# Sums of squares ahead of the input projections moved from GpSimd to TensorE, and all residual additions to VectorE

## The reference

```python
def rmsnorm(x, g):
    xf = x.astype(jnp.float32)
    y = xf * lax.rsqrt(jnp.mean(xf * xf, axis=-1, keepdims=True) + RMS_EPS)
    return (y * g.astype(jnp.float32)).astype(x.dtype)
...
    for i in range(DEPTH):
        hn = rmsnorm(x, norm_mix_pre[i])
...
        x = x + rmsnorm(m, norm_mix_post[i])
        hn = rmsnorm(x, norm_ffn_pre[i])
        f = conv_ffn(hn, ffn_w_up[i], ffn_conv_w[i], ffn_conv_b[i], ffn_w_down[i])
        x = x + rmsnorm(f, norm_ffn_post[i])
```

## Time and profile before

| | us |
|---|---|
| median of 3 runs | 1633.6 (1633.12 to 1633.71) |
| the profiled execution | 1633.11 |
| its span, first to last instruction | 1631.3 |
| mean granted TensorE clock | 0.958 of 2.4 GHz |
| boundary 0: first product to the norm's broadcast | 10.65 to 26.16 |
| boundary 1: first product to the norm's broadcast | 552.74 to 572.80 |
| boundary 2: first product | 945.51 |
| boundary 3: first product to the norm's broadcast | 1233.30 to 1253.34 |

### The profile page before, as it was taken

The page is one execution under the profiler, slowest core; times in us unless marked ns, Lnnn a source line. Parts: engine busy times, 40 slices in busy tenths (PEclk is TensorE's granted clock), DMA queues, the critical chain, the costliest instruction groups (busy, mean ns, idle before and its releaser), DMA issues.

```text
span 1631.3 us, 20778 instructions
## 1 busy us (share of the span) xinstructions
PE 1495.3 (92%) x6774; PEld 1183.5 (73%) x6774; DVE 1020.8 (63%) x1443; ACT 585.4 (36%) x832; POOL 460.9 (28%) x236
## 2 busy tenths in 40 slices
PE   6799888988699799999999979999796999999996
PEld 5577676776588578888888757777574888888885
DVE  6888888889830587777800067777608877875002
ACT  5433344333432332232222235556434223223221
POOL 4333334334345500000044552322064000000453
PEclk9899999999899899999999989999898999999998
DMA  4333231332112122322322212211021232223221
GB/s 140 120 107 113 103 128 52 116 116 103 65 65 95 47 91 90 103 90 90 107 94 98 74 39 78 65 64 64 13 90 39 91 101 91 90 95 109 89 92 66
DMA packets 36271, 142.02 MB, mean 87 GB/s; under 512 B 4048, under 2 KB 4176, under 8 KB 34192
## 3 DMA queue, kind: packets, MB, share of 16 engines
q1 hardware_dynamic: 36240, 141.62, 25.1%
HBM read 139.38 MB, written 2.23 MB: 87 GB/s over the span
## 4 chain that ended last, share of the span: by engine, by line
PE 65%; DVE 17%; issue 12%; POOL 3%; ACT 2%; DVEq 1%; DMA 0%; SPq 0%; POOLq 0%; ACTq 0%
PE bank L353 20%; PE bank L354 20%; PE bank L355 20%; DVE cv_s L650 4%; POOL w_lo L322 3%; DVE cv_s L644 2%; DVE m_t L942 2%; DVE hn_lo L531 2%; DVE mbuf L539 1%; DVE x L555 1%; PE b_x L741 1%; PE b_y L666 1%; DVE ug_s L641 1%; PE b_y L669 1%; ACT w_hi L316 1%
## 5 line engine op out<-in xcount | busy, mean ns | idle before, releaser
L322 POOL TENSOR_TENSOR w_lo<-raw,w_hi 128x1024 fp32r<-128x1024 f32 (+1 forms) x125 | 325.3, 2602 | 1055.2 <-ACT w_hi L316 1055.2
L353 PE MATMUL bank<-hn_hi,w_hi 128*128 128x512 f32 x1288 | 526.5, 409 | 41.5 <-DVE hn_lo L531 32.9
L354 PE MATMUL bank<-hn_lo,w_hi 128*128 128x512 f32 x1288 | 516.0, 401 | 0.0
L355 PE MATMUL bank<-hn_hi,w_lo 128*128 128x512 f32 x1288 | 515.5, 400 | 0.0
L316 ACT ACTIVATE w_hi<-raw 128x1024 fp32r<-128x1024 f32 (+1 forms) x217 | 239.9, 1106 | 540.8 <-PE bank L355 534.8
L353 PEld LDWEIGHTS bank<-hn_hi,w_hi 128*128 128x128 f32 x1288 | 247.3, 192 | 116.6 <-issue 30.5
L355 PEld LDWEIGHTS bank<-hn_hi,w_lo 128*128 128x128 f32 x1288 | 246.2, 191 | 59.9
L354 PEld LDWEIGHTS bank<-hn_lo,w_hi 128*128 128x128 f32 x1288 | 247.2, 192 | 56.2
L387 DVE RECIPROCAL rcol<-root 128x4 f32<-128x4 f32 x24 | 4.1, 173 | 378.5 <-ACT root L375 368.6
L355 PE MATMUL bank<-h_hi,w_lo 128*128 128x512 f32 x352 | 139.2, 396 | 0.0
L353 PE MATMUL bank<-h_hi,w_hi 128*128 128x512 f32 x352 | 139.2, 396 | 0.0
(11 more groups left out here) (185 smaller groups left out, 1796.5 us busy)
## 6 DMA issues: line engine op xcount, KB each, us to landing
raw<-w_up SPq DMA_DIRECT2D x88, 512.0 KB, 3.2
raw<-w_mix SPq DMA_DIRECT2D x49, 512.0 KB, 3.2
raw<-w_dn SPq DMA_DIRECT2D x32, 704.0 KB, 4.0
raw<-w_qkv SPq DMA_DIRECT2D x24, 512.0 KB, 3.3
acs_bc<-scratch SPq DMA_DIRECT2D x8, 1024.0 KB, 4.7
ecs_bc<-scratch SPq DMA_DIRECT2D x8, 1024.0 KB, 6.7
raw<-w_sout SPq DMA_DIRECT2D x16, 512.0 KB, 3.2
raw<-w_aout SPq DMA_DIRECT2D x8, 512.0 KB, 3.3
```

Of the source, the lines that this page charges most:

```text
L322: nc.gpsimd.tensor_tensor(w_lo[:, slot, 0:ph.width], raw[:, slot, 0:ph.width], w_hi[:, slot, 0:ph.width].bitcast(F32), ALU.subtract).then_ ...
L353: nc.tensor.matmul(acc[:], wh, hi, start=first, stop=False)
L354: nc.tensor.matmul(acc[:], wh, lo, start=False, stop=False)
L355: return nc.tensor.matmul(acc[:], wl, hi, start=False, stop=last)
```

## The change

In boundaries 0 to 3 the squares of the pre norm are no longer added up by GpSimd. Each chunk's squares go straight to TensorE: `chunk_stat` makes four matmuls of one column with `sq` as weights and adds their results up in the bank `b_cb`. It stands behind the six products of its chunk, except for chunk 7, where it stands ahead of them. `sq_added`, for which ScalarE's squares wait, now rises there, on TensorE. The root reads `b_cb`. `POOL_ADDS` is empty for boundaries 1 to 3, so VectorE makes all eight additions to x; in boundary 4 it stays as it was. TensorE's wait for the last chunk of x moves from ahead of the sum to just ahead of the broadcast. The sums of the post norms stay.

```diff
-        def norm_root(act, n):
+        def norm_root(act, n, stat=b_norm):
             act.wait_ge(stat_ready, n + 1)
-            nc.scalar.activation(root[:], b_norm[:, 0:NB], ACT.Sqrt, bias=eps[:]).then_inc(root_ready, 1)
+            nc.scalar.activation(root[:], stat[:, 0:NB], ACT.Sqrt, bias=eps[:]).then_inc(root_ready, 1)
...
+        def chunk_stat(pe, name, m):
+
+            pe.wait_ge(sq_ready, KC * sum_no[name] + m + 1)
+            for b in range(NB):
+                last = nc.tensor.matmul(b_cb[:, b:b + 1], sq[:, m % 2, b * P:(b + 1) * P], mean_col[:, 0:1],
+                                        start=m == 0 and b == 0, stop=m == KC - 1 and b == NB - 1)
+            last.then_inc(sq_added if m < KC - 1 else stat_ready, 1)
...
-        POOL_ADDS = {b: (1, 3, 5) for b in range(1, 4)}
+        POOL_ADDS = {b: () for b in range(1, 4)}
         POOL_ADDS[4] = (1, 3, 5, 6)
...
             for c in range(KC):
                 if c == KC - 1:
-                    if b:
-                        wait_x_scaled(pe, b)
-                    sum_stat(pe, f"pre{b}")
+                    chunk_stat(pe, f"pre{b}", c)
                 pe.wait_ge(hnlo_ready, KC * b + c + 1)
                 for j in range(2):
                     last = product(acc_of(nxt, j), slot_of(nxt, j), c, hn_hi[:, c, :], hn_lo[:, c, :],
                                    c == 0, c == KC - 1)
                     if c == KC - 1:
                         last.then_inc(unit_done, 1)
+                if c < KC - 1:
+                    chunk_stat(pe, f"pre{b}", c)
+            if b:
+                wait_x_scaled(pe, b)
             norm_bcast(pe, norm_no[f"pre{b}"])
...
-            norm_root(act, norm_no[f"pre{b}"])
+            norm_root(act, norm_no[f"pre{b}"], b_cb)
...
             for m in range(KC):
                 if b and m in POOL_ADDS[b]:
                     add(m)
-                if nxt is not None and m:
-                    add_square(pool, f"pre{b}", m - 1, m - 1)
```

## The result

The median of the changed kernel is 1645.0 us (6 runs, 1641.0 to 1646.4), that of the kernel before 1633.9 us in the same comparison: a ratio of 1.0061, interval 1.0047 to 1.0075. The profiled execution took 1644.46 us, 11.4 us more than that of before (1633.11), and its spans differ by as much. It is slower, but by a sixth of the 68.8 us that were forecast.

A forecast was written before the change was run, and what follows sets the result against it. TensorE bounds boundary 0; VectorE, slowed by GpSimd, is last in the others at the fast clock. Slow-clock terms 17.8 + 3 x 13.2 + 4 x 2.1 + 3 x 1.0 = 68.8 us more gave 1702.4 us, range 1641 to 1712.

The forecast's parts named there:

- the case given 0.62: Boundaries 0 to 3: the clock, slow at each start, stays slow until the last chunk; 1702.4 us, own range 1677 to 1710.
- rival 1: Boundaries 0 to 3: clock rises as before; boundary 0 +5.3 us, the others 1.5 each, 1643.4 us in total; chance 0.16.
- the 3.85 us of the sum: Boundaries 1 to 3: TensorE's waits at the fast clock, which the added blocks would fill, 3.85 us in each.
- the term of 3.0 for the slow clock: Boundary 1 before the change: what the first 6.0 us at the slow clock cost, taken as 3.0 us.
- The price of a block: Four one-column matmuls between products on TensorE: 0.89 us at the fast clock, up to 1.7 at the slow one.
- Six products alone did not raise it: Ahead of the last attention products: clock 0.50 throughout 9.2 us, with six slow products, a wait and a longer run.
- The other reading, of the one-column matmuls at boundary 4: Boundary 4: after 1.9 us of them and 1.29 us idle the next matmul is slow, so they seem to weigh little or nothing.
- the terms of 17.8 and 3 x 13.2 us: Added loop time at the slow clock: 17.8 us in boundary 0 and 13.2 us in each of boundaries 1 to 3.
- the slow chunk 7, the slow broadcasts (1.10 us) and the slow units behind them: Slow clock at loop ends: chunk 7 1.1 us more, broadcast 1.0, each boundary; next unit 1.0 behind boundaries 1 to 3.
- 31.8 us: Each changed loop, first product to the one behind the last sum: slow products and start 18.1, blocks 10.2, pair 3.5.
- rival 2: Clock rises midway in some of the four boundaries and then stays up: 1643 to 1702 us, middle 1673; chance 0.13.
- Rival 4: Blocks nearly free at 0.1 us each, TensorE's waits in boundaries 1 to 3 go: 1624.4 us; chance 0.03.

The follow-up runs named there:

- the second trace: The changed kernel itself, unmodified, measured and profiled once more: 1649.0 us, ratio 1.0080 to the kernel before.
- the doubled loop: The changed kernel with every one-column block made twice, the second into other columns of the same bank: 1684.8 us, ratio 1.0321.
- wide blocks: The changed kernel with four fp32r matmuls of 512 columns, results unused, replacing the one-column block behind each of chunks 0 to 5: 1637.5 us, ratio 1.0028.
- the last version: Changed kernel with squares of chunks 0 to 6 summed element by element by full-width fp32r identity matmuls, ScalarE copying the sum: 1620.6 us, ratio 0.9937.

## Why the prediction was wrong

The direction was right and the time lies in the range, but the size was off by a factor of six, and the case given 0.62 did not happen. That 1645 lies in 1641 to 1712 says nothing for the mechanism: the range had been drawn down to 1641 for rival 1. Step by step:

*What bounds the kernel.* Right. TensorE in boundary 0; VectorE, slowed by GpSimd, in the others at the fast clock. `hn_lo` fell to 0.75 us, and TensorE's waits are gone. They were larger than the 3.85 us of the sum, 4.4 to 4.9 by the distances between starts: the term of 3.0 for the slow clock was too high, 13 slow products cost 13 x 0.195 = 2.5. The half of it that I had not seen: GpSimd's additions and its sums each slow VectorE (`hn_lo` 1.02 beside the additions, 1.15 beside the sums). With the additions alone taken off GpSimd the loop fell by 0.5 us, with neither left and no blocks to 15.66 us; the sums alone were taken off only with the blocks in place, where TensorE is last.

*The price of a block.* Right at both clocks: 576.83 to 577.64 is 0.81, 561.35 to 562.91 is 1.56, and the start behind a slow block is 0.15 longer, 1.71 against the 1.7 that was taken as the upper bound.

*VectorE and ScalarE not last.* Right: TensorE has no idle time in any of the loops.

*The clock.* Here it failed, at the sentence "Six products alone did not raise it". It was read from one place, the last attention products, where the run of six stands next to idle time, and it was made a rule for all places. The trace of before already showed a spread: the clock rose behind 10 to 13 slow products in its own four boundaries, behind nine in one place, and behind four that follow six matmuls of 256 columns in another:

```profile
53.34 0.57 PE L353 MATMUL bank<-hn_hi,w_hi 128*128 128x512 f32 x1 [2.85 <-POOL w_lo L322]
...
57.09 0.40 PE L353 MATMUL bank<-hn_hi,w_hi 128*128 128x512 f32 x1
...
281.77 2.42 PE L741 MATMUL b_x<-xdd,btok 128*128 128x256 f32 x6 [3.17 <-DVE xdd L956]
283.63 0.99 PE L353 MATMUL bank<-hn_hi,w_hi 128*128 128x512 f32 x1
...
285.70 0.41 PE L354 MATMUL bank<-hn_lo,w_hi 128*128 128x512 f32 x1
```

In the changed loop six products raised the clock behind the first chunk in one of the four loops of the first trace, behind the second in two and behind the fourth in one; the second trace has the rise behind one, three, two and three chunks. Never did it stay low to chunk 7. The other reading, of the one-column matmuls at boundary 4, pointed the right way: the rise came later behind one-column blocks than behind wide ones, and the clock fell behind a row of them in the doubled loop. But what stands in the changed loop is a delay of the rise: from that a delay with a spread had to follow, and I turned it into a certainty for four boundaries at once. With it fell the terms of 17.8 and 3 x 13.2 us for the loops, and those of the slow chunk 7, the slow broadcasts (1.10 us) and the slow units behind them (in boundary 1 the next unit starts 2.64 us behind the broadcast, at the fast clock, as the 2.68 before). In place of 31.8 us, the product behind the last sum starts 18.4 to 24.5 us after the first (975.76 - 957.32 in boundary 2, 583.10 - 558.65 in boundary 1).

*The rivals.* What happened is rival 1 in two loops and rival 2 in the others. With two slow chunks, about what a rise takes before, the loops of boundaries 0 and 3 came out 6.24 and 2.02 us longer, where rival 1 has 5.3 and 1.5. In boundary 0 the difference is the blocks that are slow even then, one in full (0.75 us more) and one in part (0.17), which its sum of fast blocks left out. In boundary 3 such blocks (0.75 and 0.42) and two more slow products (0.4) come on top, and the waits, larger than the 3.85 that it took off, hide most of that: there its number is near for a part by luck. Boundary 1, with two chunks more, is the rival of the clock that rises midway; boundary 2 has one less. The Trainium skill's sentence in "TensorE: Matmul & The Clock Gate", section "What's actually happening", that being busy releases the throttled state, pointed to this side. The runs agree with it for full-width matmuls (with wide blocks the rise came behind 6, 9, 6 and 6 slow products), but not for one-column ones: in the doubled loop the engine was busy throughout, and its clock fell from 1.00 to 0.50. What I should have weighed is that the case needed the same outcome in four boundaries: what is likeliest for each does not make the four together likely.

*Rival 4* asked for nearly free blocks; they are not, 1.15 to 1.3 us each with their part in the clock. But what it counted on, VectorE's waits, is real, and the version with full-width additions collects it.

*What stays open.* What exactly fixes the chunk behind which the clock rises wasn't found. In all twenty loops with one-column blocks in the traces the first rise falls into a block, right behind six products, and never into the products; with wide blocks it fell into the products once in four loops. Three kernels (the changed one, the one with GpSimd's additions, the one with boundary 0 as before) had 24, 6 and 12 slow products in the boundaries 1 to 3, and the changed one's second trace 18, 12 and 18, so it isn't the code of a boundary, but three equal series make it unlikely that it is drawn anew for each boundary either. Whether the column count, the number type or the weight loads of the blocks delay the rise is open too. Nor is the split of the gain of the last version shown outside its loops: the loops are 9.2 us shorter, the profiled execution 13.7 us (1619.41 against 1633.11), the medians 9.7.

## What to carry to other kernels

Price a small TensorE operation twice: its own time, and what it does to the clock around it; four matmuls of one column cost nearly the time of four of 512 columns here (0.89 against 0.93 us), and behind them the clock rose later, so sums may be better put on the moving side at full width, even if that does much more arithmetic. With identity as weights this gained 0.6% here; with ones it gained nothing, because the reciprocal grew with it. When the price hangs on when the clock rises, take a range per place and add the ranges up; don't carry the state of one place to all. And look at all that runs beside an engine before taking one part of it away: moving GpSimd's additions to VectorE alone left the time as it was, and with the sums gone too (and not made elsewhere) each of the boundaries 1 to 3 took 4.2 to 4.4 us less.

## What the runs showed of the hardware

- The granted clock fell from 1.00 to 0.50 at the end of a loop in which TensorE was busy without a gap, behind 32 one-column matmul instructions in 3.5 us, in the six products that follow them (the doubled blocks, boundary 1). The same sequence in the boundaries 0 and 2 of that execution left it at 1.00.
- Four plain fp32 matmuls of one column with 128x128 weights, eight instructions in the trace, take 0.81 us at the fast clock and 1.56 at the slow one; where more stand in a row, each further eight take 0.89 (the pair 581.39 to 583.10, 1.71).
- A reciprocal of 128x512 on VectorE takes 3.35 us, where a multiplication of that size takes 0.69 and the reciprocal of 128x4 0.18.
- VectorE's `hn_lo` has 1.29 us with GpSimd's sums and additions in the loop, 1.15 with the sums alone, 1.02 with the additions alone, 0.75 with neither.
